# Decoder layer in split fp32: gate and up projections with the high and low activations as one 512-column operand

## What is computed

```python
def conv_glu_ffn(h, w_gate, w_up, conv_w, conv_b, w_down):
    S = h.shape[1]
    g = h @ w_gate
    u = h @ w_up
    gp = jnp.pad(g, ((0, 0), (CONV_WIDTH - 1, 0), (0, 0)))
    g = conv_b + gp[:, 0:S] * conv_w[0]
    for j in range(1, CONV_WIDTH):
        g = g + gp[:, j:j + S] * conv_w[j]
    return (jax.nn.gelu(g, approximate=True) * u) @ w_down
...
        h = rms_norm(x, ffn_pre_g[l])
        y = conv_glu_ffn(h, w_gate[l], w_up[l], conv_w[l], conv_b[l], w_down[l])
        x = x + rms_norm(y, ffn_post_g[l])
```

## Time and profile before

| | us |
|---|---|
| median of 3 runs | 1587.79 (1587.0 to 1588.45) |
| span of the profiled execution | 1584.8 |
| PE busy | 1506.7 (95%) |
| DVE busy | 900.6 (57%) |
| ACT busy | 650.9 (41%) |
| POOL busy | 182.0 (11%) |
| data moved | 276.31 MB, mean 174 GB/s |

### The profile page before, as it was taken

One profiled execution on the slowest core, in us unless ns is written; L12 is line 12 of the kernel. 1 busy time (PEld: TensorE's weight loads), 2 busy tenths in 40 slices (PEclk: granted clock), 3 DMA queues, 4 the chain that ended last, 5 costly groups with the idle time before them and its releaser, 6 DMA issues.

```text
span 1584.8 us, 27901 instructions
## 1 busy us (share of the span) xinstructions
PE 1506.7 (95%) x10336; PEld 1404.3 (89%) x10336; DVE 900.6 (57%) x1285; ACT 650.9 (41%) x780; POOL 182.0 (11%) x172
## 2 busy tenths in 40 slices
PE   5998989998789999999999999999999999999995
PEld 5988888887669999999999999999999888888884
DVE  4555565655456656666655666665566544545454
ACT  4443433444345434344333443443334444444442
POOL 0522324230000001111100111110011000000000
PEclk9999999999899999999999999999999999999998
DMA  8554545454354666666666666656665655655552
GB/s 278 180 166 136 162 136 171 127 171 133 112 170 125 200 185 182 184 183 177 181 186 185 179 180 184 183 175 185 185 185 174 193 189 192 191 190 192 189 193 84
DMA packets 126294, 276.31 MB, mean 174 GB/s; under 512 B 8976, under 2 KB 9776, under 8 KB 126000
## 3 DMA queue, kind: packets, MB, share of 16 engines
q1 hardware_dynamic: 124608, 272.66, 56.2%
q10 hardware_dynamic: 1648, 3.14, 0.5%
HBM read 273.67 MB, written 2.10 MB: 174 GB/s over the span
## 4 chain that ended last, share of the span: by engine, by line
issue 66%; PE 21%; DVE 5%; POOL 4%; ACT 3%; DMA 1%; ACTq 0%; POOLq 0%; DVEq 0%
POOL act_g L555 4%; PE bank L935 3%; PE bank L939 3%; PE bank L937 3%; PE bank L918 3%; PE bank L920 3%; PE bank L922 3%; ACT w_hi L361 2%; DVE w_lo L573 1%; DMA count_t<-in_key_count 1%; DVE probs L649 1%; PE bank L979 1%; ACT exps L383 1%; DVE row_max L640 1%; DVE masked L636 1%
## 5 line engine op out<-in xcount | busy, mean ns | idle before, releaser
L573 DVE TENSOR_TENSOR w_lo<-stage,w_hi 128x1024 fp32r<-128x1024 f32 x512 | 633.3, 1238 | 594.3 <-ACT w_hi L361 593.6
L361 ACT CAST w_hi<-stage 128x1024 fp32r<-128x1024 f32 x512 | 536.5, 1048 | 724.9 <-PE bank L922 423.2
L918 PE MATMUL bank<-hT_lo,w_hi 128*128 128x256 f32 x2560 | 730.7, 285 | 1.0 <-DVE w_lo L573 1.0
L920 PE MATMUL bank<-hT_hi,w_hi 128*128 128x256 f32 x2560 | 725.6, 283 | 0.0
L922 PE MATMUL bank<-hT_hi,w_lo 128*128 128x256 f32 x2560 | 725.4, 283 | 0.0
L918 PEld LDWEIGHTS bank<-hT_lo,w_hi 128*128 128x128 f32 x2560 | 492.7, 192 | 1.6 <-issue 1.2
L920 PEld LDWEIGHTS bank<-hT_hi,w_hi 128*128 128x128 f32 x2560 | 492.7, 192 | 0.4
L922 PEld LDWEIGHTS bank<-hT_hi,w_lo 128*128 128x128 f32 x2560 | 492.5, 192 | 0.0
L1089 PE MATMUL bank<-w_hi,a_hi 128*128 128x512 f32 x512 | 159.5, 393 | 0.0
L1089 PE MATMUL bank<-w_hi,a_lo 128*128 128x512 f32 x512 | 158.3, 390 | 1.0 <-DVE aT L822 1.0
L1089 PE MATMUL bank<-w_lo,a_hi 128*128 128x512 f32 x512 | 158.6, 391 | 0.0
(11 more groups left out here) (99 smaller groups left out, 820.7 us busy)
## 6 DMA issues: line engine op xcount, KB each, us to landing
stage<-in_w_gate SPq DMA_DIRECT2D x128, 512.0 KB, 3.7
stage<-in_w_up SPq DMA_DIRECT2D x128, 512.0 KB, 3.7
stage<-in_w_down SPq DMA_DIRECT2D x128, 512.0 KB, 4.7
stage<-in_w_qkv SPq DMA_DIRECT2D x96, 512.0 KB, 3.7
stage<-in_w_o SPq DMA_DIRECT2D x32, 512.0 KB, 3.8
resid<-in_x SPq DMA_DIRECT2D x4, 512.0 KB, 7.3
out<-y_out SPq DMA_DIRECT2D x8, 256.0 KB, 3.4
post_g<-in_attn_post_g ACTq DMA_DIRECT2D x1, 1024.0 KB, 14.8
```

The costliest lines, as they stand in the source:

```text
L361: nc.scalar.copy(w_hi[s][:, :], stage[s][:, :]).then_inc(s_hi, 1)
L573: nc.vector.tensor_tensor(w_lo[s][:, :], stage[s][:, :], w_hi[s][:, :].bitcast(F32), ALU.subtract).then_inc(s_lo, 1)
L918: nc.tensor.matmul(o, w_hi[s][:, w], hT_lo[:, k, :], start=(k == 0 and j % 2 == 0), stop=False, skip_group_check=True)
L920: nc.tensor.matmul(o, w_hi[s][:, w], hT_hi[:, k, :], start=False, stop=False, skip_group_check=True)
```

## The change

`hT_hi` and `hT_lo` become the two halves of one tile `hT` [128, 16, 2, 256], so that for one k-tile they are 512 neighbouring columns. `split_unit` takes the place of `column_unit` in gate and up: one 512-column matmul of w_hi with both halves, and one 256-column matmul of w_lo with the high half, into the second half of the same bank. Each column tile now fills a bank: gate is in banks 0 to 3, up in 4 to 7. DVE adds the halves of a bank with a reduce over pairs, then scales (gate, in place) or multiplies with the gelu (up, through a new tile `up_sum`); PE's waits for free banks go by the reduces. In iteration 0 the row norm is made earlier, and the broadcast comes before unit 8 with a wait of PE for its copy. Iteration 1 is unrolled on ACT and DVE as well. Down's banks are swapped, so that its unit 0 uses the former gate banks.

```diff
-        hT_hi = sb("hT_hi", [P, KT, SEQ], F32R)
-        hT_lo = sb("hT_lo", [P, KT, SEQ], F32R)
+        hT = sb("hT", [P, KT, 2, SEQ], F32R)
+        hT_hi, hT_lo = hT[:, :, 0, :], hT[:, :, 1, :]
...
+        up_sum = sb("up_sum", [P, SEQ])
...
-        GATE_BANK, UP_BANK = 0, 2
+        GATE_BANK, UP_BANK = 0, 4
...
@@ scalar
-                if n == 8:
+                if n == 4:
                     act.wait_ge(s_resid, OUT_CHUNKS * TT)
                     residual_sumsq()
...
@@ vector, take_gate
-                nc.vector.tensor_tensor(gate[:, :], bank[GATE_BANK + j // 2][:, (j % 2) * SEQ:(j % 2 + 1) * SEQ],
-                                        rms_bc[:, :], ALU.mult).then_inc(s_gate_out, 1)
+                nc.vector.tensor_reduce(gate[:, :], bank[GATE_BANK + j][:, :].rearrange("p (h t) -> p t h", h=2),
+                                        AX_X, ALU.add).then_inc(s_gate_out, 1)
                 dve.wait_ge(s_gate_out, f + 1)
+                chain.link(nc.vector.tensor_tensor(gate[:, :], gate[:, :], rms_bc[:, :], ALU.mult))
+                chain.settle()
...
@@ vector, take_up
-                dve.wait_ge(s_gelu_rms, i * CT + j + 1)
-                nc.vector.tensor_tensor(aT[:, bass.ds(i * CT + j, 1), :],
-                                        bank[UP_BANK + j // 2][:, (j % 2) * SEQ:(j % 2 + 1) * SEQ],
+                f = i * CT + j
+                if not (isinstance(i, int) and i == 0 and j == 0):
+                    dve.wait_ge(s_up_out, f)
+                nc.vector.tensor_reduce(up_sum[:, :], bank[UP_BANK + j][:, :].rearrange("p (h t) -> p t h", h=2),
+                                        AX_X, ALU.add).then_inc(s_up_sum, 1)
+                dve.wait_ge(s_up_sum, f + 1)
+                dve.wait_ge(s_gelu_rms, f + 1)
+                nc.vector.tensor_tensor(aT[:, bass.ds(f, 1), :], up_sum[:, :],
                                         act_g[:, j, :], ALU.mult).then_inc(s_up_out, 1)
...
@@ vector, iterations
-                if n == 9:
+                if n == 6:
                     dve.wait_ge(s_sumsq, 2 * TT)
                     mean_square(D)
+                if n == 7:
+                    diagonals(4)
                 if n == 10:
-                    diagonals(4)
-                if n == 11:
                     keep_broadcast(3, rms_bc, S_BANK)
                     dve.wait_ge(s_bc_copied, 4)
                 take_gate(0, n)
-            with dve.Fori(1, F_ITERS) as i:
-                chain.enter(i, 1, 2 * CT)
+            def ffn(i):
                 for n in range(F_UNITS):
                     low_part(i * (F_UNITS // RING) + F_START // RING + n // RING, n % RING)
                     take_up(i - 1, n)
                     take_gate(i, n)
+            ffn(1)
+            with dve.Fori(2, F_ITERS) as i:
+                chain.enter(i, 2, 3 * CT)
+                ffn(i)
...
@@ tensor
+            def split_unit(rnd, s, kp, first_bank):
+                pe.wait_ge(s_lo, 4 * rnd + s + 1)
+                for kk in range(2):
+                    k = 2 * kp + kk
+                    for j in range(CT):
+                        w = slice(kk * CHUNK + j * P, kk * CHUNK + (j + 1) * P)
+                        nc.tensor.matmul(bank[first_bank + j][:, :], w_hi[s][:, w], hT[:, k, :, :],
+                                         start=(k == 0), stop=False, skip_group_check=True)
+                        ins = nc.tensor.matmul(bank[first_bank + j][:, SEQ:2 * SEQ], w_lo[s][:, w],
+                                               hT_hi[:, k, :], start=False, stop=(k == KT - 1),
+                                               skip_group_check=True)
+                ins.then_inc(s_used, 1)
...
+                    if first and n == CHUNK_UNITS:
+                        pe.wait_ge(s_hT_lo, 2 * KT)
+                        broadcast(3, S_BANK)
+                        pe.wait_ge(s_bc_copied, 4)
                     if not first and n == CHUNK_UNITS:
-                        pe.wait_ge(s_up_out, i * CT)
-                    column_unit(i * (F_UNITS // RING) + F_START // RING + n // RING, n % RING,
-                                n % CHUNK_UNITS, (GATE_BANK, UP_BANK)[n // CHUNK_UNITS])
+                        pe.wait_ge(s_up_sum, i * CT)
+                    split_unit(i * (F_UNITS // RING) + F_START // RING + n // RING, n % RING,
+                               n % CHUNK_UNITS, (GATE_BANK, UP_BANK)[n // CHUNK_UNITS])
...
-                    if first and n == 9:
-                        broadcast(3, S_BANK)
...
+                    if first and n == 0:
+                        pe.wait_ge(s_gate_out, FT)
                     if first and n == 1:
-                        pe.wait_ge(s_up_out, FT)
+                        pe.wait_ge(s_up_sum, FT)
```

More of the change, by code:

```diff
@@ L234, in layer_kernel @@
         s_y_out = sem("y_evacuated")
+        s_up_sum = sem("up_summed")
         s_gate_out = sem("gate_evacuated")
@@ L484, in _ @@
                 ffn_gelu(0, n)
-            with act.Fori(1, F_ITERS) as i:
+            def ffn(i):
                 for n in range(F_UNITS):
@@ L488, in _ @@
                     ffn_gelu(i, n)
+            ffn(1)
+            with act.Fori(2, F_ITERS) as i:
+                ffn(i)
             def down(i):
@@ L509, in _ @@
                 for t in range(TT):
-                    y_squares(c, t, (4 if c < 2 else 0) + 2 * (c % 2) + t, s_d_sq)
+                    y_squares(c, t, 2 * c + t, s_d_sq)
         @block.gpsimd
@@ L848, in _ @@
                     take_gate(i, n)
-            chain.leave(F_ITERS - 1)
+            ffn(1)
+            with dve.Fori(2, F_ITERS) as i:
+                chain.enter(i, 2, 3 * CT)
+                ffn(i)
+            chain.leave(F_ITERS - 2)
             def down(i):
@@ L872, in _ @@
                     dve.wait_ge(s_d_sq, c * TT + t + 1)
-                    nc.vector.tensor_tensor(y_out[:, t, cs], bank[(4 if c < 2 else 0) + 2 * (c % 2) + t][:, :],
+                    nc.vector.tensor_tensor(y_out[:, t, cs], bank[2 * c + t][:, :],
                                             ffn_g[:, cs], ALU.mult).then_inc(s_d_out, 1)
@@ L1089, in down @@
                                 ins = nc.tensor.matmul(
-                                    bank[(4 if half == 0 else 0) + 2 * c + t][:, :], a[kk][:, k, ts],
+                                    bank[4 * half + 2 * c + t][:, :], a[kk][:, k, ts],
                                     w[s][:, c * CHUNK:(c + 1) * CHUNK],
```

## The result

| | median us | runs | range |
|---|---|---|---|
| before | 1587.58 | 9 | 1586.03 to 1589.21 |
| after | 1580.07 | 9 | 1564.4 to 1587.38 |

The ratio is 0.9935, with a 95% interval of 0.9909 to 0.9961. The forecast was 1566.5, and the gain is a third of the one forecast (7.5 against 21.3 us). That the time lies in the range given (1560 to 1582) is luck: the range reached so far for rival (b), a slower reduce (1579.3), and the reduce is not slower. The runs of after spread far wider than those of before: 1564.4 and 1565.2, one at 1587.4, the other six at 1577.9 to 1581.0.

The account below looks back on a forecast made before the run. PE bounds the kernel, by matmuls times spacing. -27.3 (wider matmuls) + 4.2 (border) + 1.0 (clock) + 0.8 (head) = -21.3 us, from 1587.8 to 1566.5 us; range 1560 to 1582, own bounds 1562 to 1572.

Parts of the forecast that it names:

- rival (b): DVE's reduce in gate and up takes one step more per output, 0.90 us: 1579.3 us; chance 12%.
- What bounds the kernel: Gate and up, and down: PE busy throughout at full clock, so time is matmuls times spacing and nothing else.
- 1. Fewer, wider matmuls: Gate and up: three 256-column matmuls per block become one of 512 and one of 256, 0.3600 to 0.3467 us; 27.3 us off.
- part 5: Head of gate and up: PE waits before unit 8 for DVE's copy of the scale row, +0.8 us; ACT's moved squares hidden.
- The bound of 25.0: Lower gain for the wider matmuls in gate and up, 25.0 us, using the down stage's 0.2278 us per matmul.
- 2. VectorE work: Gate and up: DVE's new reduce over 512 elements takes 0.66 us, assuming that reading pairs 1 KB apart is free.
- (a): Pairs cost double, reduce 1.14 us, DVE becomes the bound inside each burst in the loop: 1593.6 us, slower; chance 10%.
- 3. The burst: Gate and up loop, units 11 to 14: DVE's step of 4.17 us fits under the limit 4.20; nothing lost.
- 4. The border: Border to down: PE waits longer for up tiles and late low half 3, +4.2 us, plus +1.0 for the fallen clock.
- Rival (d): Gate and up: narrow matmul behind a wide one into the same bank spaces out; gain 0 to 10, 1584 to 1594; 6%.

Follow-up runs that it names:

- VA: PE-alone bench kind computing nothing of the layer: as V4 (value projection's order, activations hT, bank 4), but with banks alternating; 226.7 ns a matmul.
- DH: PE-alone bench kind computing nothing of the layer: down's order with its activations in the place of hT instead of the arena; 226.7 ns a matmul.
- the kernel with the border edit: Changed kernel with wide and narrow matmuls skewed, plus the last four up reduces, then their multiplies, ahead of low part 3 at the border to down: 1572.68 us.

## Why the prediction was right in its frame and wrong in its size

**What bounds the kernel** held. PE's time in gate and up is matmuls times spacing: with DVE at 72% instead of 58 no wait appeared in the loop, and the version with the wide matmul taken apart shows that only PE's spacing moves that stage.

**1. Fewer, wider matmuls: the step that failed.** "Both are (columns + 32)" was read off two uniform streams and applied to a mixed one. Uniform streams on the bench do give 226.7 and 120.0. Alternating, the pair is 353.3 in both traces of this program, not 346.7: 2048 x 6.7 ns = 13.7 us off instead of 27.3. (Gate and up got 12.3 shorter, not 13.7: 0.5 of the rest is the wait of part 5, and 0.5 is unit 0, which began further from the clock's rise and took 4.13 instead of 3.61.) The sentence on the bounds held a clue that was taken for noise: down's 0.2278 against the value projection's 0.2267 isn't a worse reading of the same spacing but another spacing, 0.2289 by the starts from 1230 to 1530 us, because the stationary operand lies elsewhere; that successive matmuls add into one bank, the reason given for choosing 0.2267, plays no part (VA 226.7, DH 226.7). A spacing that differs with an address was a reason not to count on 0.3467 to a tenth of a ns. The bound of 25.0 drawn from it was far too near: mixed streams were not bounded at all, and the nearest end was no gain per matmul (0.360).

**2. VectorE work** held: 683 ns for the reduce against 660, so pairs 1 KB apart cost DVE hardly more than the line through the contiguous reduces (653). Rivals (a), 1140 ns, and (b), 900 ns, are out. The Trainium skill's rule that each two consecutive elements in PSUM should be contiguous ("Advanced Engine Details and Errata", "PSUM Cachelines") shows no such penalty on this read.

**3. The burst** fits: the step is 4.06 us against 4.17 (the limit of 4.20 is 4.30 with units of 2.83) and PE waits for no low half. Of the two register waits of 0.18 us only one is there: between reduce and in-place multiply the gap is 0.04 (1002.67 + 0.68 to 1003.39); the 0.19 is at the next instruction.

**4. The border**: right in sum (+5.2 as forecast), by terms that missed both ways. Unit 1 starts 1210.69 - 1203.71 = 6.98 after unit 0, +3.0 against 3.94 before, where +4.2 were forecast: low half 3 wasn't late, it begins 1.34 after PE's start as before, since low half 15 ended 3.8 us ahead of that start and not 2.96. The clock cost 2.2 instead of 1.0: the loss had been counted over the 4 us of the earlier trace rows alone, while here the clock stays at 0.50 until 4.8 us after PE goes on. In the traces of three other kernels with the same border it cost 1.4 to 1.6.

**5. The head**: wait of 0.5 against 0.8. The move of the squares on ACT was hidden as forecast.

**The sum** with the measured terms: -13.7 + 3.0 + 2.2 + 0.5 = -8.0, so 1579.8 by the forecast's base; measured 1580.07 and 1578.87. The forecast's own lower bound was added up wrongly: 1566.5 less 1.5, 1.0 and 0.5 is 1563.5, not 1562. Rival (d) had the right place, the spacing of wide and narrow matmuls in turn, but not the size: it gave the spacing a gain of 0 to 10 us, where 13.7 were measured, so its 1584 to 1594 missed too, and its reason (two matmuls into the same bank) is excluded by the benches. It deserved more than 6%: nothing in the trace before shows wide and narrow matmuls in turn, and the whole gain was 13 ns in 360. The 70% of the forecast were too many for the same reason.

**Left open.** What draws the level, 346.7 or 353.3, of an alternating stream. Out as its sole cause are other engines and DMA (both levels come with PE alone), the clock's fall and return (both levels come behind long and short gaps), the bank, and which half of it is written. No trace of the whole kernel at the fast level was caught; that the three executions near 1565 are such is argued from their distance alone. The runs at 1573.0 and 1587.4 fit neither level and aren't explained.

## What to carry to other kernels

Where a stage is a count of matmuls times their spacing, a gain of a few ns per matmul is only as sure as the spacing of that very sequence: widths in turn have to be timed as they will run, and one trace of them isn't enough, since the same instructions can run at two levels. Prefer an order with one level (here runs of two wide and two narrow), and try the address of the stationary operand. Where DVE gains work, put what PE waits for ahead of what it doesn't at each stage border: there 4 us of wait also cost 1.4 to 2.2 us of clock.

## What the hardware showed that was not expected

- A matmul of 512 columns for which PE waits on nothing was 226.7, 228.9 or 233.3 ns apart from the next, in long uniform streams. The first two go by the stationary operand's place: 226.7 at 64, 114 and 122 KB of a partition's SBUF, 228.9 at the places tried from 139 KB on. The output projection (from 420 us on) ran at 233.3 in the trace of the kernel with the border edit and at 228.9 in those of the other kernels with the change, by the same code in the same place; in both traces with the layout of before, 1 KB lower, at 233.3.
- Wide and narrow in turn ran at 346.7 or 353.3 ns a pair on the bench; in the two traces of the change it kept 353.3 to the end of a stream of over 700 us. In runs of two it was 348.4 in all 12 bursts on the bench and 348.3 in the one trace of the kernel.
- The Trainium skill, page "TensorE: Matmul & The Clock Gate", section "Back-to-back issue gap", gives N/2.4 + 2.5 ns for an isolated matmul at full clock. By it a pair would be an estimated 325 ns; no alternating stream here came under 346.7, so the measurement decides.
